# Expert rounds: selection turned one step later in another bank, last activations turned by TensorE

## What is computed

```python
def swiglu(h, wg, wu, wd):
    return (jax.nn.silu(h @ wg) * (h @ wu)) @ wd

def moe_swiglu(h, w_router, wg, wu, wd):
    t = h.reshape(-1, shp[-1])                       # 256 tokens x 1024
    top_v, top_i = lax.top_k(t @ w_router, TOP_K)    # 2 of 8 experts
    gates = jax.nn.softmax(top_v, axis=-1)
    for e in range(N_EXPERTS):
        w_e = jnp.sum(jnp.where(top_i == e, gates, 0.0), axis=-1)
        out = out + w_e[:, None] * swiglu(t, wg[e], wu[e], wd[e])
```

## Time and profile before

| | us |
|---|---|
| median of 3 runs | 1900.63 (1897.96 to 1901.6) |
| the profiled execution, device time | 1901.12 |
| its span, first to last instruction | 1899.0 |
| TensorE busy | 1755.5 (92%) |
| VectorE busy | 1015.5 (53%) |
| ScalarE busy | 457.9 (24%) |
| mean DMA rate over the span | 256 GB/s |

### The profile page before, as it was taken

One profiled execution on the slowest core, in us unless ns is written; L12 is line 12 of the kernel. 1 busy time (PEld: TensorE's weight loads), 2 busy tenths in 40 slices (PEclk: granted clock), 3 DMA queues, 4 the chain that ended last, 5 costly groups with the idle time before them and its releaser, 6 DMA issues.

```text
span 1899.0 us, 23610 instructions
## 1 busy us (share of the span) xinstructions
PE 1755.5 (92%) x9665; PEld 1052.6 (55%) x9666; DVE 1015.5 (53%) x1749; ACT 457.9 (24%) x782; POOL 413.1 (22%) x233
## 2 busy tenths in 40 slices
PE   5999988989999999999888998999989999987797
PEld 2777556868788888788655343333433454332332
DVE  4864765656634344540363865444665556655433
ACT  4343256642222222342361101000000000100011
POOL 1431562432444443444540000000000000000000
PEclk8999998999999999999999999999999999998899
DMA  9345000234555551346309999799979999899996
GB/s 371 131 179 198 23 1 2 90 125 143 199 178 183 197 197 67 108 103 167 90 24 375 383 425 415 325 402 403 426 322 426 425 427 414 365 426 426 425 388 259
DMA packets 105736, 485.69 MB, mean 256 GB/s; under 512 B 26512, under 2 KB 53569, under 8 KB 77949
## 3 DMA queue, kind: packets, MB, share of 16 engines
q1 hardware_dynamic: 105144, 483.02, 64.7%
q10 hardware_dynamic: 453, 0.65, 0.1%
HBM read 482.57 MB, written 1.07 MB: 255 GB/s over the span
## 4 chain that ended last, share of the span: by engine, by line
PE 63%; DVE 9%; DMA 4%; issue 2%; ACT 1%; POOL 0%; DVEq 0%; SPq 0%; ACTq 0%; POOLq 0%
PE PS L2828 17%; PE PS L2858 11%; PE PS L2630 5%; PE PS L2631 5%; PE PS L2634 5%; DMA BIG<-in_od_exp_wu 4%; PE PS L2842 4%; PE PS L2222 3%; PE PS L2223 3%; PE PS L2224 3%; DVE ZS L2117 3%; PE PS L2748 1%; PE PS L2792 1%; DVE X L1763 1%; DVE PS L2083 1%
## 5 line engine op out<-in xcount | busy, mean ns | idle before, releaser
L2828 PE MATMUL PS<-BIG,QB 128*64 128x448 f32 x1152 | 225.8, 546 | 14.7 <-issue 7.7
L766 POOL TENSOR_TENSOR BIG_parts<-BIG,QB_parts 128x2048 fp32r<-128x2048 f32 x33 | 156.7, 4749 | 229.8 <-ACT QB_parts L934 229.6
L2858 PE MATMUL PS<-BIG,ZS 128*64 128x512 f32 x840 | 187.6, 599 | 11.9 <-DVE YB L2106 9.8
L1336 ACT ACTIVATE QB<-PS 64x448 f32<-64x448 f32 x64 | 34.7, 542 | 645.7 <-PE PS L2828 645.6
L2828 PEld LDWEIGHTS PS<-BIG,QB 128*64 128x64 f32 x1152 | 83.4, 138 | 152.5 <-issue 150.3
L766 POOL TENSOR_TENSOR BIG_parts<-BIG,BIG_parts 128x2048 fp32r<-128x2048 f32 (+1 forms) x25 | 114.6, 4585 | 151.0 <-ACT BIG_parts L934 143.3
L2630 PE MATMUL PS<-HB_parts,QB_parts 128*128 128x512 f32 (+1 forms) x384 | 140.9, 373 | 0.4 <-issue 0.4
L2858 PEld LDWEIGHTS PS<-BIG,ZS 128*64 128x64 f32 x840 | 64.7, 138 | 126.3 <-issue 121.8
L2117 DVE STREAM_TRANSPOSE ZS<-MOD 32x224 f32<-32x224 f32 x224 | 128.9, 576 | 3.3
L2117 DVE STREAM_TRANSPOSE ZS<-CM 32x224 f32<-32x224 f32 x224 | 128.8, 575 | 3.3
L2828 PE MATMUL PS<-BIG,HB 128*64 128x448 f32 x608 | 124.3, 565 | 6.1 <-issue 4.8
(11 more groups left out here) (434 smaller groups left out, 3306.1 us busy)
## 6 DMA issues: line engine op xcount, KB each, us to landing
BIG<-in_od_exp_wg SPq DMA_DIRECT2D x55, 1792.0 KB, 16.4
BIG<-in_od_exp_wu SPq DMA_DIRECT2D x55, 1792.0 KB, 20.2
BIG<-in_od_exp_wd SPq DMA_DIRECT2D x50, 1792.0 KB, 18.2
BIG<-in_ada_w SPq DMA_DIRECT2D x24, 2048.0 KB, 8.0
QB<-in_od_exp_wg SPq DMA_DIRECT2D x9, 1792.0 KB, 16.1
XT<-in_od_exp_wu SPq DMA_DIRECT2D x9, 1792.0 KB, 20.0
QB<-in_od_exp_wd SPq DMA_DIRECT2D x7, 1792.0 KB, 9.7
XT<-in_od_exp_wd SPq DMA_DIRECT2D x7, 1792.0 KB, 13.5
```

Of the source, the lines that this page charges most:

```text
L766: pool.tensor_tensor(r12(w), w, r12(high), ALU.subtract).then_inc(split_l, 1)
L2828: last = mm(PS[64 * u:64 * u + 64, c, 0:GROUP], XGS[x][:, 4 * part + k, 0:64], wgu[u][:, k, GROUP * c:GROUP * c + GROUP], start=(part + k ...
L2858: last = mm(PS[64 * n:64 * n + 64, bank, :], HET[:, s % 2, k, r0:r0 + 64], half[:, a, :], start=(k == 0), stop=(k == 6))
```

## The change

It has three parts.

1. In rounds 0 to 5 the four transposes of SEL1 move from step 1 to step 2, and write bank 4 and not bank 6. The wait for e_add moves from ahead of them to the end of step 1, ahead of `down(0)`. The wait for their copy (e_trev) moves from ahead of `down(0)` to the end of the round. ScalarE's copy and VectorE's `select` for the next round move to step 2 with them.
2. In rounds 0 to 5 the last step's activations are turned as in round 7: seven TensorE transposes, and one ScalarE copy. VectorE's 16 transposes of that step go. In rounds 0, 1 and 3 the seven stand between two gathers and the other two; in round 5, ahead of the last `down`.
3. VectorE also zeroes four blocks of 32 partitions x 128 elements of DINV[0] and EINV[1].

```diff
@@ ScalarE, wave
                 def hidden_columns(s):
-                    act.wait_ge(e_htr, NPAIR * w + s + 1)
+                    act.wait_ge(e_htr, NPAIR * w + s + 1 if alone else ROUNDS.index((w, nx)) + 1)
...
-                    if s == 1:
+                    if s == (1 if alone else 2):
                         if not opening:
                             act.wait_ge(e_sc, 4 * w + 4 * nx)
                         act.wait_ge(e_tr, w + nx)
-                        act.activation(SELT, PS[:, 6, :].rearrange("p (a b) -> p a b", a=4), ACT.Copy).then_inc(e_trev, nx)
+                        act.activation(SELT, PS[:, 6 if alone else 4, :].rearrange("p (a b) -> p a b", a=4),
+                                       ACT.Copy).then_inc(e_trev, nx)
...
-                if alone:
-                    hidden_columns(NPAIR * nx - 1)
+                hidden_columns(NPAIR * nx - 1)
@@ VectorE
             for v in EINV[0] + DINV[1]:
-                last = dve.memset(v, 0.0)
+                dve.memset(v, 0.0)
+            for v in range(2):
+                dve.memset(DINV[0][v][0:32, :, 32:64], 0.0)
+                last = dve.memset(EINV[1][v][96:P, :, 64:96], 0.0)
...
+                        if c == 0 and own is None and s == 1 and not opening:
+                            dve.wait_ge(e_htr, ROUNDS.index((w, nx)))
...
-                    if own is None:
+                    if own is None and s + 1 < NPAIR * nx:
                         hidden_columns(w, s, opening)
                     if s:
                         take_down(w, s - 1, nx)
-                    if s == 1 and following:
+                    if s == 2 and following:
@@ TensorE, wave
-                        if s == 1 and part == 0:
-                            if not opening:
+                        if s == (1 if own else 2) and part == 0:
+                            if own:
                                 pe.wait_ge(e_add, 8 * w + 8 * nx)
                             pe.wait_ge(e_sel, 4 * w + 4 * nx)
                             for t in range(4):
-                                last = pe.transpose(PS[:, 6, t * P:t * P + P], SEL1[:, t, :], ident())
+                                last = pe.transpose(PS[:, 6 if own else 4, t * P:t * P + P], SEL1[:, t, :], ident())
                             last.then_inc(e_tr, nx)
...
-                    if s == 1:
+                    if s == 1 and own:
                         pe.wait_ge(e_trev, w + nx)
+                    elif s == 1 and not opening:
+                        pe.wait_ge(e_add, 8 * w + 8 * nx)
                     if s:
                         down(s - 1)
...
-                if own:
-                    columns(NPAIR * nx - 1)
+                if not own:
+                    pe.wait_ge(e_trev, w + nx)
+                columns(NPAIR * nx - 1)
                 if following:
-                    pe.wait_ge(e_h, NGR * w + 2 * NPAIR * nx)
                     gather(0, 1, 1)
                     gather(1, 1, 3)
                 down(NPAIR * nx - 1)
```

## The result

| | before | after |
|---|---|---|
| median of 4 runs each, us | 1901.12 (1897.96 to 1904.45) | 1885.29 (1883.29 to 1886.77) |
| the profiled execution | 1901.12 | 1884.93 |
| its span | 1899.0 | 1882.9 |
| TensorE busy | 1755.5 | 1755.2 |
| VectorE busy | 1015.5 | 984.6 |

The ratio is 0.9915, 95% interval 0.9898 to 0.9931. The kernel gained 16 us, not the 27 predicted, and 1885.3 lies above the range.

The account below looks back on a forecast made before the run. TensorE and weight transfers bound the expert stage in turns, with 41.7 us of dry queue. Loads' lead grew 8.3, 14.9, 23.1, then 4.0 more to 27.1 us: 1873.5 us from the median, range 1869 to 1883.5.

Parts of the forecast that it names:

- The zeroed blocks: Four small VectorE memsets, hidden by 3.67 us of idle time: cost 0, at most 2.1 us.
- The selection, moved: Step 1 stops of rounds 1, 3, 5 vanish, giving TensorE 7.6, 7.7, 7.2 us; no wait ahead of `down(0)`.
- C: Stretch 1340 to 1430 us, where the weight queue was dry for 11.6 us; loads predicted 14.9 us earlier at its slot.
- The last step's activations: Ends of rounds 0, 1, 3, 5: TensorE's lead changes by + 0.7, - 1.1, + 2.8, + 9.7 us.
- A: Stretch 1120 to 1240 us, where the weight queue was dry for 12.7 us, more than the 8.3 us lead.
- the rival: TensorE's transposes at round ends bring the half clock, matmuls behind lose 2.1 us: 1882.0 us; chance 0.08.
- T: TensorE's lead against its old times: 17.7 us after round 3, 23.2 at round 5's slot load.
- D: Stretch 1570 to 1640 us, where the weight queue was dry for 8.2 us, all predicted to be filled.
- Q: The loads' lead against their old times, limited by TensorE's lead and dry time passed: 27.1 us at the end.
- What follows the last weights is unchanged: End of kernel: last `down` comes right behind the last weights, so the loads' whole 27.1 us lead reaches the end.
- E: Stretch 1810 to 1850 us, where the weight queue was dry for 4.0 us, predicted to be filled.
- the first half: Selection move without the activations' gain: 20.8 us, 1879.8 us; rival that the second half (activations) yields nothing, chance 0.12.

Follow-up runs that it names:

- pad5_64: Changed kernel plus 32 never-executed transposes (64 instructions) in a skipped block of round 5's last step: 1877.34 us, ratio 0.987.
- nojump: Changed kernel with all never-entered code for additional rows left out of all rounds: 1873.83 us, ratio 0.9842.
- nojump7: Changed kernel with the never-entered code for additional rows left out of round 7 only: 1874.18 us, ratio 0.9843.
- before_nojump7: Kernel before the change, with round 7's never-entered code for additional rows left out: 1899.49 us, ratio 0.9978.
- before_pad56: Kernel before the change plus 28 never-executed transposes (56 instructions) in a skipped block of round 5's last step: 1907.41 us, ratio 1.0028.
- sel_only: Kernel before with the selection moved and the zeroed blocks, but last-step activations still turned by VectorE: 1879.07 us, ratio 0.9867.

## Why the prediction was right in its mechanism and wrong in its size

**The zeroed blocks: right.** They take 0.17 us each, and VectorE's idle time behind them shrinks from 3.67 to 2.86. VectorE in time order:

```profile
306.44 2.11 DVE L1650 MEMSET BIG<- 128x512 f32 x4 [0.38 <-DVE YB L1623]
308.51 0.17 DVE L1652 MEMSET BIG<- 32x128 f32 x1
...
312.22 2.22 DVE L1674 STREAM_TRANSPOSE BIG<-BIG 32x128 f32<-32x128 f32 x7 [2.86 <-ACTq L1108]
```

**The selection, moved: right.** The stops in step 1 are gone. TensorE in round 1 goes from part 1 straight to `down(0)`:

```profile
1161.95 6.18 PE L2833 MATMUL PS<-BIG,HB 128*64 128x448 f32 x32
1167.96 2.32 PE L2863 MATMUL PS<-BIG,ZS 128*64 128x512 f32 x10
```

VectorE's last addition ends at 1167.10 (1166.41 + 0.69) and `down(0)` starts at 1167.96, so the cover was 0.9 us where 1.2 were worked out. At C, SP issues at 1390.61 and not at 1405.72: 15.1 us earlier, 14.9 predicted. This execution also reached the experts 0.9 us later (first gather at 1035.62 and not 1034.7), which lies in the spread of all kernels' profiles, 1034.0 to 1037.9.

**The last step's activations: right in each round.** Seven transposes take 1.02 us between the gathers (1.13 predicted), and the wait of 9.77 is 1.26. TensorE at the ends of rounds 3 and 5:

```profile
1552.17 3.84 PE L2797 MATMUL PS<-QB,X 128*128 128x128 f32 x32
1555.85 1.02 PE L2825 MATMUL PS<-CM,MOD 128*128 128x128 f32 x7
1556.70 3.74 PE L2797 MATMUL PS<-QB,X 128*128 128x128 f32 x32
...
1747.45 1.13 PE L2825 MATMUL PS<-CM,MOD 128*128 128x128 f32 x7
1749.84 6.23 PE L2863 MATMUL PS<-BIG,ZS 128*64 128x512 f32 x28 [1.26 <-ACT ZS L1342]
```

The transposes brought no half clock with them: the 28 matmuls behind take 6.23. Neither did the clock fall without the stops (1.00 in A and C). In the last round the rival isn't quite refuted. In pad5_64 a wait of 1.97 us behind seven transposes leaves 32 matmuls at 7.93 us, while in after waits of 1.75 and 2.08 us behind other work leave the matmuls at full speed (28 in 5.48, the 32 of the gather in 3.83).

The order that the Trainium skill gives in VectorE: DVE Perf Modes, "The three transpose paths", for bf16 (390 ns on TensorE, 311 ns on VectorE) is the other way round for these 32-bit tiles: seven transposes and the wait for ScalarE's copy take 1.13 and 1.26 us, VectorE's 16 took 9.4 us.

**T between C and D: the first step that failed.** The prediction has 17.7 after round 3 and 23.2 at the slot of D. Two waits for instructions stand in between, one in round 3 and one at the start of round 5. TensorE in time order:

```profile
1508.07 1.01 PE L2833 MATMUL PS<-QB 128*64 128x448 f32 x1 [2.33 <-issue]
...
1581.12 5.48 PE L2833 MATMUL PS<-BIG,QB 128*64 128x448 f32 x28 [1.75 <-issue]
...
1593.60 12.25 PE L2833 MATMUL PS<-BIG,HB 128*64 128x448 f32 x64
```

The kernel before had one of 1.81 in round 3 (at 1474.10) and full speed behind it. Part 1 of step 1 of round 5 starts at about 1599.8, half way through the last row, and not at 1619.39: 19.6 earlier, 3.6 short. Q at D, by SP's issue, is 1621.17 - 1600.61 = 20.6 and not 23.1, and 70 x 16/426 = 2.6 us of D stay dry (410 GB/s). By SP's issues the lead grew by 20.6 - 15.1 = 5.5 us between C and D, where 8.2 were predicted. The two waits less the one of before are 2.33 + 1.75 - 1.81 = 2.3 us of these 2.7. The prediction had put the waits for instructions at nothing new. nojump, without those two waits, has D full.

**"What follows the last weights is unchanged": the second, and larger.** E was filled as predicted, and the last weights but two came 24.7 us earlier (27.1 predicted: 2.5 less at D). The end came 16.0 us earlier. The tail between them grew by 8.7 us. In it and just ahead of it stand the two late pieces, 4.49 and 4.40, with slow matmuls behind both (8.79 for 29 and 7.93 for 32). At full clock these take about 5.67 and 6.23, so the two cost TensorE some 13.7 us, and the tail grew by 8.7. The rest can fall where TensorE would have waited for weights; nojump7 waits 5.01 for them there, at 1827.09.

**Why it wasn't foreseen.** The page had a warning: "issue" ends most of the idle time of L2828 before, 7.7 of 14.7 us. It was a weak one, for 4.22 of the 7.7 have no instruction packet and lie where TensorE waits for weights; 1.81 and 1.69 are waits for instructions. I read the stops that other engines end, and took the rest for constant. The change was costed by time and by wait, and not by the place of the code behind it. With that disturbance out (nojump7 against before_nojump7) the gain is 25.7 us, which is near the predicted 27. That is in part luck: the first half gives 21.7 of it and the second 4.0, where the sum had 20.8 and 6.3.

**What stays open.** That a piece of program is asked for late, and waits among weight packets, is put together from four things shown: each such wait ends 1.2 to 1.6 us behind the landing of an instruction packet, the waits go with the blocks, move with the code, and shrink with the load. The 4.40 us part into 1.85 before the packet's record starts, 1.07 for the packet, and 1.48 until TensorE goes on. Whether the 1.85 us are late asking or standing in the queue, no run shows. Why before_pad56 pays 1.74 where after pays 4.49 isn't settled. Nor is it why the landing of nojump is 1.9 us earlier than that of nojump7 and its time is not.

## What to carry to other kernels

Where transfers fill the DMA queues, a branch over a large block that is never entered is not free for TensorE: the waits behind it were 1.1 to 7.0 us here, depending on where the code lies and how long the leap is, and were gone or 0.16 us with the queues at 42 GB/s. They don't all reach the end, and an edit can be charged for instructions that it merely moved. When a change gives less than its sum, compare the waits that the profile calls "issue", look whether a packet of the instruction queue lands in them, and shift the code by some never-executed instructions, which leaves the work as it is. A lead that an engine wins is worth only the dry time of the queue that is still ahead: the 9.7 us won 100 us before the end were worth some 2 to 4.

## What the runs showed of the hardware

- The 40 waits for instructions of over 1 us in the profiles end 1.2 to 1.6 us behind the landing of a packet of the instruction queue.
- 64 TensorE instructions that never run made the kernel faster by 8 us (1885.3 to 1877.3; ratios 0.9915 and 0.987). 56 of them made the kernel before slower, by 0.28%.
- With 256 instructions between them (200 added to the 56 of the change) the pattern of waits in the last round is again that of the kernel before; with 56 and with 120 it is another. This fits pieces of 256 instructions, which at 16384 bytes a packet would be 64 bytes each (an estimate).
- The same program at the same places paid 4.49 and 4.40 us with the queues at 425 GB/s, and 0 and 0.16 us at 42 GB/s (one run).
- TensorE worked from 1120 to 1430 at a granted clock of 1.00 without the two stops it had before.
- The fastest kernels with all the code in them are sel_only and pad5_64 (ratios 0.9867 and 0.987), both ahead of the change as it was made (0.9915).
